# Splitting the low parts of streamed weights between VectorE and GpSimd in a hybrid encoder layer

## The reference, cut to what matters

```python
x = x + 0.5 * swiglu_ffn(rms_norm(x, ffn1_norm[l]), ffn1_w_in[l], ffn1_w_out[l])     # D_FF = 2816
h = rms_norm(x, mix_norm[l])
q, k, v, xr, gate = jnp.split(h @ w_in_proj[l], ...)
y_attn = diff_attention(q, k, v, ...)      # 4 heads, two softmax maps a head
y_rnn = rg_lru_branch(xr, gate, ...)       # convolution, gates, scan
x = x + jnp.concatenate([y_attn, y_rnn], axis=-1) @ w_out_proj[l]
x = x + 0.5 * swiglu_ffn(rms_norm(x, ffn2_norm[l]), ffn2_w_in[l], ffn2_w_out[l])
```

## Time and profile before

| | us |
|---|---|
| runs, median of 3 | 938.45 |
| the profiled execution, whole | 938.35 |
| its span from the first to the last instruction | 936.5 |
| TensorE matmul busy | 922.3 (98% of the span) |
| VectorE busy | 482.4 (52%) |
| ScalarE busy | 331.1 (35%) |
| GpSimd busy | 3.1 (0%) |
| granted TensorE clock, mean | 1.000 |

### The profile page before, as it was taken

How to read it: one execution, slowest core, us unless ns; L and a number is a source line. 1 busy time by engine, 2 the same in 40 slices (tenths; PEclk the granted TensorE clock), 3 DMA queues, 4 the chain that set the end, 5 groups by cost and what they waited for, 6 DMA issues and landing times.

```text
span 936.5 us, 11101 instructions
## 1 busy us (share of the span) xinstructions
PE 922.3 (98%) x4154; PEld 754.2 (81%) x4154; DVE 482.4 (52%) x712; ACT 331.1 (35%) x526; POOL 3.1 (0%) x25
## 2 busy tenths in 40 slices
PE   8999999999999999999997999999999999999998
PEld 7888888888888888777885678888888888888887
DVE  6754444444444346665879776645444444422221
ACT  7422222332223233356647654332222233211220
POOL 0000000000000000000000000000000000000000
PEclk9999999999999999999999999999999999999999
DMA  7222222222222224222221022322233222132241
GB/s 272 97 90 95 113 106 90 90 90 76 90 95 92 92 95 154 97 83 90 91 90 45 1 91 70 111 90 90 90 105 119 90 90 76 63 122 92 92 140 42
DMA packets 16295, 89.13 MB, mean 95 GB/s; under 512 B 2064, under 2 KB 2192, under 8 KB 8976
## 3 DMA queue, kind: packets, MB, share of 16 engines
q1 hardware_dynamic: 16128, 88.32, 27.1%
q0 software_dynamic: 144, 0.52, 0.2%
HBM read 86.74 MB, written 2.10 MB: 95 GB/s over the span
## 4 chain that ended last, share of the span: by engine, by line
PE 95%; DVE 2%; ACT 1%; DMA 1%; issue 1%; SPq 0%; ACTq 0%
PE bank L975 31%; PE bank L977 30%; PE bank L976 30%; PE bank L1172 1%; PE bank L1115 1%; PE bank L1149 1%; DMA raw<-w_in_dram 1%; PE bank L1162 0%; PE bank L1089 0%; DVE h_lo L599 0%; DVE small L896 0%; ACT w_hi L341 0%; PE bank L990 0%; ACT sq L518 0%; DVE yr_lo L803 0%
## 5 line engine op out<-in xcount | busy, mean ns | idle before, releaser
L975 PE MATMUL bank<-h_hi,w_hi 128*128 128x512 f32 x768 | 301.4, 392 | 0.9 <-DVE w_lo L587 0.8
L977 PE MATMUL bank<-h_hi,w_lo 128*128 128x512 f32 x768 | 298.9, 389 | 0.0
L976 PE MATMUL bank<-h_lo,w_hi 128*128 128x512 f32 x768 | 298.9, 389 | 0.0
L587 DVE TENSOR_TENSOR w_lo<-raw,w_hi 128x1024 fp32r<-128x1024 f32 (+1 forms) x178 | 188.7, 1101 | 79.5 <-ACT w_hi L341 73.9
L341 ACT ACTIVATE w_hi<-raw 128x1024 fp32r<-128x1024 f32 (+1 forms) x178 | 160.9, 951 | 159.9 <-PE bank L977 159.9
L975 PEld LDWEIGHTS bank<-h_hi,w_hi 128*128 128x128 f32 x768 | 144.1, 188 | 32.9 <-DVE w_lo L587 1.2
L976 PEld LDWEIGHTS bank<-h_lo,w_hi 128*128 128x128 f32 x768 | 144.2, 188 | 30.9 <-issue 1.2
L977 PEld LDWEIGHTS bank<-h_hi,w_lo 128*128 128x128 f32 x768 | 144.2, 188 | 30.1
L975 PE MATMUL bank<-act_hi,w_hi 128*128 128x512 f32 x352 | 136.9, 389 | 0.0
L976 PE MATMUL bank<-act_lo,w_hi 128*128 128x512 f32 x352 | 136.9, 389 | 0.0
L977 PE MATMUL bank<-act_hi,w_lo 128*128 128x512 f32 x352 | 136.9, 389 | 0.0
(11 more groups left out here) (173 smaller groups left out, 656.7 us busy)
## 6 DMA issues: line engine op xcount, KB each, us to landing
raw<-w_in_dram SPq DMA_DIRECT2D x43, 1024.0 KB, 4.8
raw<-w_out_dram SPq DMA_DIRECT2D x32, 704.0 KB, 4.0
raw<-w_qkv_dram SPq DMA_DIRECT2D x6, 1024.0 KB, 4.8
raw<-w_rnn_dram SPq DMA_DIRECT2D x4, 1024.0 KB, 4.7
raw<-w_proj_dram SPq DMA_DIRECT2D x4, 1024.0 KB, 4.8
x<-xT_dram SPq DMA_DIRECT2D x8, 256.0 KB, 6.0
out_dram<-x SPq DMA_DIRECT2D x8, 256.0 KB, 5.0
raw<-w_in_dram SPq DMA_DIRECT2D x4, 256.0 KB, 6.0
```

The source lines that it names most:

```text
L587: dve.tensor_tensor(w_lo[:, part], raw[:, part], w_hi[:, part].bitcast(F32), ALU.subtract).then_inc(low_made, 1)
L975: pe.matmul(dst, s_hi, m_hi, start=first, stop=False)
L976: pe.matmul(dst, s_hi, m_lo, start=False, stop=False)
L977: return pe.matmul(dst, s_lo, m_hi, start=False, stop=last)
```

## The change

GpSimd subtracts the second half of the low part of every chunk from chunk 1 on, VectorE only the first half. The halves have a semaphore each: `low_made` counts VectorE's (one for a chunk, where it was two), `low_second` GpSimd's. GpSimd waits for the second high half of the chunk (`high_made`), subtracts and raises `low_second`. Whoever waited for `low_made` alone (SP before a load, TensorE before a chunk) waits for both. GpSimd's older work (the load of `bd`, `mask`, the margins of `xrp`) stands between its halves of chunk `C_RNN` and chunk `C_RNN + 1`. Chunk 0 is as before.

```diff
             def load(w, n, c, slot, size, first=False):
                 if not first:
-                    sp.wait_ge(low_made, c * 2 - 2)
+                    sp.wait_ge(low_made, c)
+                    sp.wait_ge(low_second, c)
...
+            sp.wait_ge(quarter_low, 2)
             with sp.Fori(1, FFN_IN // 2) as i:
...
         def _(pool):
             pool.sem_inc(chunk_used, 2)
             pool.sem_inc(u_scaled, 2)
+            pool.sem_inc(low_second, 2)
...
+            def second_lows(c, slot, size):
+                part = slice(slot * SLOT + size // 2, slot * SLOT + size)
+                pool.wait_ge(high_made, c * 2 + 2)
+                pool.tensor_tensor(w_lo[:, part], raw[:, part], w_hi[:, part].bitcast(F32), ALU.subtract).then_inc(low_second, 1)
+
+            pool.wait_ge(consts_made, CONSTS_FIRST)
+            second_lows(1, 1, IN_COLS)
+            for c0, count, size in ((C_IN1 + 2, FFN_IN - 2, IN_COLS), (C_OUT1, FFN_OUT, OUT_COLS)):
+                with pool.Fori(0, count // 2) as i:
+                    for s in range(2):
+                        second_lows(i * 2 + (c0 + s), s, size)
+            second_lows(C_RNN, 0, IN_COLS)
             pool.wait_ge(chunk_used, USED(C_RNN - 1))
             pool.dma_start(bd[:, :], bd_in).then_inc(bd_landed, 16)
...
+            pool.wait_ge(consts_made, CONSTS_ALL)
+            second_lows(C_RNN + 1, 1, IN_COLS)
+            for c0, count, size in ((C_RNN + 2, C_IN2 + FFN_IN - C_RNN - 2, IN_COLS), (C_OUT2, FFN_OUT, OUT_COLS)):
+                with pool.Fori(0, count // 2) as i:
+                    for s in range(2):
+                        second_lows(i * 2 + (c0 + s), s, size)
...
             def lows(c, slot, size):
 
-                for j in range(2):
-                    part = slice(slot * SLOT + j * size // 2, slot * SLOT + (j + 1) * size // 2)
-                    dve.wait_ge(high_made, c * 2 + (j + 1))
-                    dve.tensor_tensor(w_lo[:, part], raw[:, part], w_hi[:, part].bitcast(F32), ALU.subtract).then_inc(low_made, 1)
+                part = slice(slot * SLOT, slot * SLOT + size // 2)
+                dve.wait_ge(high_made, c * 2 + 1)
+                dve.tensor_tensor(w_lo[:, part], raw[:, part], w_hi[:, part].bitcast(F32), ALU.subtract).then_inc(low_made, 1)
...
+            def split_done(c):
+                pe.wait_ge(low_made, c + 2)
+                pe.wait_ge(low_second, c + 2)
...
                 def in_step(i, s, meanwhile=None):
-                    pe.wait_ge(low_made, i * 4 + 2 * ((C_IN1, C_IN2)[f] + s + 1))
+                    split_done(i * 2 + ((C_IN1, C_IN2)[f] + s))
```

More of the change, by code:

```diff
@@ L200, in build @@
         low_made = sem("low_made")
+        low_second = sem("low_second")
         chunk_used = sem("chunk_used")
@@ L292, in _ @@
             sp.wait_ge(stored, 16 * KT)
+        CONSTS_FIRST = 2 + ROPE_HALF + 2
+        CONSTS_ALL = CONSTS_FIRST + 2 + 4
         @block.gpsimd
@@ L320, in _ @@
                 pool.memset(mask[r:r + 1, P:P + 64], NEG_INF).then_inc(consts_made, 1)
-        CONSTS_FIRST = 2 + ROPE_HALF + 2
-        CONSTS_ALL = CONSTS_FIRST + 2 + 4
+            pool.wait_ge(consts_made, CONSTS_ALL)
[4 more added lines that the diff above has]
+                        second_lows(i * 2 + (c0 + s), s, size)
         @block.scalar
@@ L1007, in first_step @@
                         if f == 1 and k % (KT // 2) == 0:
-                            pe.wait_ge(low_made, 2 * c0 + 1 + k // (KT // 2))
+                            pe.wait_ge(low_second if k else low_made, c0 + 2)
                         if k == 0:
@@ L1040, in ffn @@
                         s, half = j // 2, j % 2
-                        pe.wait_ge(low_made, i * 8 + 2 * ((C_OUT1, C_OUT2)[f] + j + 1))
+                        split_done(i * 4 + ((C_OUT1, C_OUT2)[f] + j))
                         if half == 0:
@@ L1066, in token_chunk @@
                 c = C_QKV + 2 * s + half
-                pe.wait_ge(low_made, 2 * (c + 1))
+                split_done(c)
                 for t in range(TT):
@@ L1095, in recurrent @@
                 if gate == 0:
-                    pe.wait_ge(low_made, 2 * (C_RNN + t + 1))
+                    split_done(C_RNN + t)
                     if t >= 2:
@@ L1180, in project @@
                 if jj == 0:
-                    pe.wait_ge(low_made, 2 * (C_PROJ + q + 1))
+                    split_done(C_PROJ + q)
                 if j == 0:
```

## The result

The changed kernel takes 943.93 us (median of 5 executions, 942.68 to 944.68), the kernel before, run beside it on the same chip, 938.74 us (5 executions, 938.32 to 939.67). The ratio is 1.0053, with a 95% interval of 1.0039 to 1.0068: slower by 5 us. The forecast was 942.0 us with a range of 938.6 to 943.2, so the direction was right, the forecast too low by 1.9 us, and the measured time outside the range by 0.7. A second set of 6 executions gave 943.65 us.

The account below looks back on a forecast made before the run. TensorE was taken to bound the kernel, its matmuls busy 922.3 of 936.5 us, so only its waits count. Losses of 1.0 + 0.4 + 2.2 = 3.6 us on 938.35 gave 942.0 us, range 938.6 to 943.2.

Parts of the forecast that it names:

- nothing to win in the loops: Steady loops: GpSimd's half is ready by 49.2 to 51 us, wanted at 53.7, so nothing gained or lost.
- TensorE's added waits: Some 90 more semaphore waits, one for each chunk: taken as 0, upper bound 0.9 us.
- A half on GpSimd: A GpSimd subtraction takes 2.2 us for 1024 columns (0.94 to 2.6) and 1.5 us for 704.
- Exclusion: GpSimd and VectorE cannot read SBUF at once; the second to come waits, at most one whole half, 2.2 us.
- Beginning: Chunk 1's second half comes late from GpSimd; TensorE starts it at 20.6 instead of 19.57: 1.0 us lost.
- unit 4: Attention: GpSimd's half delays VectorE's L911 by 0.9 us, of which 0.4 us reach TensorE; bounds -0.2 and 0.9.
- end: End of attention: GpSimd's half cuts in before head 3 of `o` is scaled: 2.2 us lost, bounds 0 and 2.6.
- GpSimd comes last in the burst: Rival, chance 0.22: at the end of attention queued head 3 precedes GpSimd, costing 0.3 us there; 940.05 us in all.
- No meeting costs anything: Rival, chance 0.20: both engines read side by side, only the beginning changes; 939.15 us, or 937.85 at fill rate.
- GpSimd is kept out while VectorE has anything queued: Rival, chance 0.10: in the beginning GpSimd passes only after five additions, chunk 1 5.9 us late; 944.7 us.
- The sum: Beginning, unit 4 and end of attention add 1.0 + 0.4 + 2.2 = 3.6 us to 938.35: 942.0 us, chance 0.45.

Follow-up runs that it names:

- e3: Changed kernel with second halves of chunks 1, C_PROJ + 1 and C_PROJ + 2 back on VectorE, other 86 on GpSimd: 938.72 us, ratio 1.0000.
- e11: Kernel of e3 with the high and low parts of the recurrent branch's output moved to the pause before attention, as in e10: 936.30 us, ratio 0.9972.
- e9: Changed kernel where GpSimd, for chunk C_PROJ + 2 alone, fills 3072 unused columns instead of subtracting; that half is left out: 943.08 us, ratio 1.0043.
- e2: Changed kernel with the second low half of chunk 1 made by VectorE again: 941.09 us, ratio 1.0040.
- e5: The changed kernel itself run again, nothing altered: 943.65 us over 6 executions, ratio 1.0050 to the kernel before.
- e13: The kernel of e2 run once more, chunk 1's second half on VectorE: 943.31 us, ratio 1.0052.
- e1: Changed kernel with the second low half of chunk C_PROJ + 2 made by VectorE again: 940.29 us, ratio 1.0017.
- e6: Kernel before with two extra VectorE scalings, 1.2 us, between its low halves of chunk 1, without GpSimd: 939.94 us, ratio 1.0018.
- e12: Kernel before with four extra VectorE scalings, 2.1 us, between heads 2 and 3 of `o`, without GpSimd: 941.70 us, ratio 1.0035.
- e7: Changed kernel: TensorE waits later for chunk 1's second half, root and reciprocal precede chunk 2's parts, GpSimd's C_PROJ + 2 half follows the scalings: 942.49 us, ratio 1.0045.
- e8: Kernel before with later wait for chunk 1's second half, and root and reciprocal ahead of chunk 2's parts: 941.43 us, ratio 1.0033.
- e10: Kernel before with high and low parts of the recurrent branch's output moved from attention units 0 and 1 to the pause before attention: 936.22 us, ratio 0.9974.

## Why the prediction was right, and where it was wrong

**What bounds the kernel; nothing to win in the loops: right.** e3 equals the kernel before, the steps are at 10.88 us, and TensorE's added waits cost nothing. VectorE's freed 94 us had no taker, shown by e3 and once more by e11.

**A half on GpSimd, 2.2 us: right, a little low.** 53 of the 57 halves of 1024 columns take 2.37 to 2.50 us, most of those of 704 columns 1.73 (forecast 1.5). That is near the upper bound of 2.6 us from three passes. The estimate from the Trainium skill's figure in the prediction was 2.25; the trace is 5 to 11% above it.

**Exclusion, taken as likeliest without a row for it: right.** L932 and L963 each wait for the end of GpSimd's subtraction, and e9 shows that it is the reading.

**Beginning 1.0, unit 4 0.4, end 2.2: right.** Measured 1.17, 0.46 and 2.15, together 3.8 instead of 3.6; 2.6 us for the last two alone in the profile of e2.

**The rivals.** "GpSimd comes last in the burst" falls with the 4.65 us of the scalings. "No meeting costs anything" falls with them and with the 1.42 us of L932. "GpSimd is kept out while VectorE has anything queued" falls with the scalings too, since head 3 stood queued right behind head 2. But what the first of these rivals describes does happen elsewhere: at 471.36, before attention, four queued instructions of VectorE pass ahead of GpSimd (the last section has the rows). Why GpSimd gets in at one border of VectorE's instructions and not at another stays open. The prediction had no reason for its choice at the end of attention beyond the order of the programs, so that part was luck, and nearly 2 us hung on it.

**The sum: the step that failed.** It counted each pause of TensorE at its length, and had no term for the clock. All rows of before were at full clock, and the prediction took it for granted that matmuls behind a new pause run at 0.227 us as well. Behind the pauses that the change makes, they sometimes don't: in the changed kernel's profile seven matmuls at 0.427 instead of 0.227 us and two partly slowed cost 1.3 us net behind the first pause (also seen in e9, 1.2), and in e5 and e13 a fall behind the late one costs 1.6. Taken over the profiles, the pause of the beginning (1.75 to 2.15 us: after, e1, e5, e6, e9) has a fall behind it in 2 of 5, the late one of 2.1 us (after, e2, e5, e12, e13) in 2 of 5. The pauses before chunk 2 in e7 (1.94 us) and e8 (2.87 us, the longest of all) have none. A fall in attention is not new in itself: e3, e8 and e12 have one without any of the three meetings, and the mean clocks of the kernel before, of which only 16 in 60 are 1.0, are read most simply as such falls. Its double length in after and e9 is seen only where the beginning had a fall as well. The forecast was made against a profile of before without any. Of the 1.9 us between forecast and median, 0.4 are this base (938.35 against the median of 938.74), 0.2 the terms, and 1.3 what came beyond the meetings. The range ended at 943.2 since it held only the bounds of the halves' durations; with one fall of 1.3 us behind a new pause its end would have been 944.5, and would have held the median.

**What is shown and what stays open.** Shown: in the profiled executions all that goes beyond the meetings (2.6 us at 944.68, 1.95 at 944.11) is lost in stretches at 1.2 GHz; the pauses alone, at full clock, give the forecast's time; and the same pause is followed by a fall in one execution and not in another. Made likely, not shown: that the pauses cause the falls. For it speak their place, within 1.2 us behind the pause of the beginning or the late one, and e10 and e11, where the waits for the maps are shorter and 13 of 16 executions are at full clock, against 16 of 60. Against it, for the pause of the beginning, speak e1 and e6, which have that pause and not the late one: only 4 of their 22 executions lie 1.3 us or more above those at full clock. Open: what decides it in a given execution, and whether GpSimd's reading plays a part in it. In e6 and e12, which make the pauses without GpSimd, no profile caught a fall behind them, but each was profiled once, which at 2 in 5 proves nothing; e12's slower executions went untraced.

## What to carry to other kernels

Work that moves to an idle engine also leaves the order of the old engine's program: what used to come behind a burst now runs into it, so look at the moment when its input is ready and at what the other engine is doing just then. Time freed on an engine is worth only what the bound engine waits for it; moving four small steps out of a stretch with such waits (e10) gave 2.4 us, moving 94 us of work away gave none. A new pause of the bound engine may have two prices, its length and a fall of the clock behind it, and the second belongs at least in the range: 1.3 to 1.6 us a fall here where the matmuls are dense.

## What the runs showed of the hardware

- **VectorE's one-input scaling is shut out too.** `xc = xrp * cols`, f32 in SBUF, 0.54 us each before, takes 2.63 us beside GpSimd's subtractions, while instructions with one input in PSUM and one in SBUF keep their 0.69 us. I had counted only instructions with two SBUF inputs; these four (the group's count, busy us and mean ns are shown) lie off the path. The section of the Trainium skill named above has `tensor_scalar` among the operations that can contend in this way; the trace agrees.

```profile
L793 DVE TENSOR_SCALAR xc<-xrp,cols 128x512 f32<-128x512 f32 x4 | 10.5, 2626 | 0.0
```

- **GpSimd waits too, and not always one instruction only.** Before attention a half takes 4.47 us instead of 2.4. It starts inside VectorE's subtraction (471.02 to 472.24), then four two-input instructions of VectorE follow at their usual 0.42 us, and only the one behind them (L871, 0.42 us when nothing comes in) is held up for 2.50. In the scalings of `o` GpSimd got in at the first border. The loops would have borne 4.47 us (they have 5 to spare).

```profile
471.36 4.47 POOL L322 TENSOR_TENSOR w_lo<-raw,w_hi 128x1024 fp32r<-128x1024 f32 x1 [10.38 <-ACT w_hi L363]
...
471.02 1.22 DVE L608 TENSOR_TENSOR w_lo<-raw,w_hi 128x1024 fp32r<-128x1024 f32 x1
472.15 0.42 DVE L868 TENSOR_TENSOR a_s<-kn,cos 128x256 f32<-128x256 f32 x1
...
473.16 0.42 DVE L868 TENSOR_TENSOR a_s<-kn,sin 128x256 f32<-128x256 f32 x1
473.62 2.50 DVE L871 TENSOR_TENSOR kn<-a_s 128x256 f32<-128x256 f32 x1
```

- **One program has times 3 us apart.** The changed kernel ran at 942.0 and at 945.6 us, and e2 and e13, the same kernel, had medians of 941.1 and 943.3. A median of 5 executions of a kernel with such pauses is no better than about 1 us here.
